# A hybrid decoder layer on one core: the 24 gate tiles shared out between sample attention, prompt attention and recurrent block

## The reference

```python
p = _split_proj(jnp.einsum('btd,de->bte', h, lw['w_in']) + lw['b_in'])
o_a = nsa(...)       # compressed, selected and window attention, 8 heads
o_b = _rglru(...)    # recurrent block: conv, gates, scan over time
o_c = _gla(...)      # gated linear attention

def _merge(o_a, o_b, o_c, gate_pre, w_branch, w_out):
    u = jnp.einsum('btzc,zcd->btzd', jnp.stack([o_a, o_b, o_c], axis=2), w_branch)
    g = jax.nn.sigmoid(gate_pre.reshape(B, T, N_BRANCH, D_MODEL))
    return jnp.einsum('btd,de->bte', jnp.sum(g * u, axis=2), w_out)

def _mlp(h, w1, w2):
    a = jax.nn.relu(jnp.einsum('btd,df->btf', h, w1))
    return jnp.einsum('btf,fd->btd', a * a, w2)
```

## Time and profile before

| | us |
|---|---|
| median of 3 runs (2349.26 to 2356.98) | 2355.3 |
| the profiled execution, its own time | 2354.62 |
| its span | 2353.0 |
| TensorE busy | 2128.4 (90%) |
| VectorE busy | 852.0 (36%) |
| ScalarE busy | 694.6 (30%) |
| GpSimd busy | 330.6 (14%) |

### The profile page before, as it was taken

The page is one execution under the profiler, slowest core; times in us unless marked ns, Lnnn a source line. Parts: engine busy times, 40 slices in busy tenths (PEclk is TensorE's granted clock), DMA queues, the critical chain, the costliest instruction groups (busy, mean ns, idle before and its releaser), DMA issues. The chain is left out here.

```text
span 2353.0 us, 36411 instructions
## 1 busy us (share of the span) xinstructions
PE 2128.4 (90%) x14280; PEld 1439.2 (61%) x14280; DVE 852.0 (36%) x1636; ACT 694.6 (30%) x1279; POOL 330.6 (14%) x245
## 2 busy tenths in 40 slices
PE   3888966799999999897699979895999999999998
PEld 2446634577777777664366756563666666666666
DVE  4211051455555555455432544334222222222223
ACT  5212231245454545326142233212211111211121
POOL 3200032400000000000102111102510410411400
PEclk7898978899999999898799989996999999999999
DMA  5421352111111111201110155302111111111101
GB/s 207 127 71 46 128 149 71 49 50 43 55 38 56 55 47 38 74 23 36 38 45 9 63 145 151 134 12 54 45 54 45 53 48 50 45 53 45 53 27 74
DMA packets 189719, 153.31 MB, mean 65 GB/s; under 512 B 9169, under 2 KB 176231, under 8 KB 189291
## 3 DMA queue, kind: packets, MB, share of 16 engines
q1 hardware_dynamic: 180170, 138.96, 19.6%
q0 software_dynamic: 4640, 10.60, 1.7%
q10 hardware_dynamic: 4800, 2.30, 0.3%
HBM read 124.66 MB, written 31.33 MB: 66 GB/s over the span
## 5 line engine op out<-in xcount | busy, mean ns | idle before, releaser
L416 PE MATMUL ps<-hH,wH 128*128 128x352 f16 x1536 | 318.3, 317 | 47.7 <-ACTq L389 27.8
L416 PE MATMUL ps<-hL,wH 128*128 128x352 f16 x1536 | 317.5, 316 | 0.0
L416 PE MATMUL ps<-hH,wL 128*128 128x352 f16 x1536 | 316.5, 315 | 0.0
L403 DVE SCALAR_TENSOR_TENSOR wL<-w,wH 128x1024 f16<-128x1024 f32 x98 | 120.1, 1225 | 323.8 <-ACT wH L396 308.3
L416 PEld LDWEIGHTS ps<-hH,wH 128*128 128x128 f16 x1536 | 151.4, 99 | 132.8 <-issue 48.5
L416 PE MATMUL ps<-mH,wH 128*128 128x352 f16 x960 | 195.9, 313 | 8.4 <-DVEq L389 6.9
L416 PEld LDWEIGHTS ps<-hL,wH 128*128 128x128 f16 x1536 | 152.1, 99 | 82.1
L416 PEld LDWEIGHTS ps<-hH,wL 128*128 128x128 f16 x1536 | 151.7, 99 | 81.3
L416 PE MATMUL ps<-mL,wH 128*128 128x352 f16 x960 | 195.9, 313 | 0.0
L416 PE MATMUL ps<-mH,wL 128*128 128x352 f16 x960 | 195.9, 313 | 0.0
L485 PE MATMUL ps<-hH,wH 128*128 128x352 f16 x576 | 181.0, 314 | 2.0 <-ACT cmpT L497 0.8
(11 more groups left out here) (409 smaller groups left out, 2929.3 us busy)
## 6 DMA issues: line engine op xcount, KB each, us to landing
w<-in_mlp_w SPq DMA_DIRECT2D x64, 512.0 KB, 3.9
w<-in_w_in SPq DMA_DIRECT2D x32, 512.0 KB, 3.9
gates<-cmpT SPq DMA_DIRECT2D x24, 528.0 KB, 3.0
hH<-gates SPq DMA_DIRECT2D x24, 528.0 KB, 3.5
paw<-in_w_in SPq DMA_DIRECT2D x24, 512.0 KB, 4.7
hL<-in_w_branch SPq DMA_DIRECT2D x24, 256.0 KB, 3.8
xTd<-xT SPq DMA_DIRECT2D x1, 4224.0 KB
xT<-xTd SPq DMA_DIRECT2D x1, 4224.0 KB, 13.0
```

Source lines behind the costliest of these rows:

```text
L403: self.k.nc.vector.scalar_tensor_tensor(self.k.wL[:, slot % 2, :, :], self.k.w32[:, slot, :, :], WS, self.k.wH[:, slot % 2, :, :], ALU.mul ...
L416: ins = nc.tensor.matmul(k.ps[:, 3 * parity + c, 0:CH], w[:, kt, :], x[:, kt, c * CH:(c + 1) * CH], start=(kt == 0 and x is inH and w is w ...
```

## The change

The 24 gate tiles are divided: tiles 0 to 3 are a `Fill` in `sample_attention`, tiles 4 to 19 the `Fill` of `prompt_attention`, and tiles 20 to 23 become four more tiles of the `Dense` of `lru`.

In `sample_attention` the fill's raw weights lie in the buffer of `k.toep` (the table of the relative bias), so the load of `toep` moves from `project_nsa` to the end of `sample_attention`. TensorE issues 4 fills after each group of key transposes, a chunk of 24 at each of the two waits for the softmax, one (first half) or two (second half) chunks ahead of the value products, and one after the first half's value products. ScalarE splits the first two tiles ahead of its first key copy; VectorE makes their low halves ahead of its other preparations. Bank 6 is now the fill's, so the small transposes go to the end of bank 7.

In `prompt_attention` the pieces follow the slots' sizes: `even_pieces` gives slot j a piece so that 3 x (tiles of jobs j, j + 2, j + 4) + 4 x piece is nearly level, and a piece never goes past a chunk's end. The pieces are 0 to 20 matmuls: the first 48 slots are 11, 10, 3, 18, 6, 13, 9, 2, 17, 7, 9, 9, 6, 9, 8, 7, 7, 6, 7, 4, 8, 5, 6, 5, 5, 5, 4, 4, 5, 1, 7, 4, 4, 3, 4, 2, 4, 3, 4, 2, 3, 3, 2, 3, 2, 8, 5, 8.

In `lru` the gate tiles are staged in the free part of `oH` and `oL` and stored by SyncE; the linear attention's ScalarE waits for these stores before it overwrites that part. SyncE loads the block-diagonal weights `gw` earlier, and `load_ahead` of the next stage and the four small outputs stand behind evictions of the gate tiles.

```diff
@@ sample_attention
+        raw = k.toep[:, :, :].rearrange("p h n -> p (h n)").rearrange("p (s kt n) -> p s kt n", s=2, kt=KD)
+        fill = Fill(k, "sf", 0, FILL_SAMPLE, raw, k.cmpT, 6)
+        PIECE, CHUNK = KD // 2, 3 * KD
...
+            fill.load(sp, 0)
+            fill.load(sp, 1)
             for b in range(NB):
+                if b == 4:
+                    fill.load(sp, 2)
+                    fill.load(sp, 3)
+                if b == NB - 1:
+                    fill.store(sp, 0)
...
+            fill.store(sp, 1)
+            sp.wait_ge(fill.lo, FILL_SAMPLE)
+            sp.dma_start(k.toep[:, :, :], ...).then_inc(s["toep"], 16)
+            for i in range(2, FILL_SAMPLE):
+                fill.store(sp, i)
+            fill.all_stored(sp)
+            sp.wait_ge(s["toep"], 16)
@@ TensorE
                         ins.then_inc(s["kturn"], 1)
+                        fill.multiply(pe, PIECE)
...
+                fill.multiply(pe, CHUNK)
                 pe.wait_ge(s["csoft"], hf + 1)
...
+                fill.multiply(pe, CHUNK)
                 pe.wait_ge(s["ccopy"], hf + 1)
...
+                fill.multiply(pe, CHUNK * (hf + 1))
                 pe.wait_ge(val_in[hf], 16 * (9 - VA) * HS)
...
                 ins.then_inc(s["o"], 1)
+                if not hf:
+                    fill.multiply(pe, CHUNK)
@@ ScalarE
+                    if b == 0:
+                        fill.split_hi(act, 0)
+                        fill.split_hi(act, 1)
+                    elif b == HS:
+                        fill.evacuate(act, 5)
...
+                    if b % 2:
+                        fill.evacuate(act, 6 * hf + b % HS // 2)
+                    if b == HS:
+                        fill.split_hi(act, 3)
                 act.wait_ge(s["cprep"], 2 * hf + 2)
...
+                fill.evacuate(act, 6 * hf + 2)
+                if not hf:
+                    fill.split_hi(act, 2)
@@ prompt_attention
-    PIECES = ((8, 0), (8, 0), (8, 1), (8, 0), (8, 0), (8, 1), (12, 0), (12, 1))
+def even_pieces(tiles, chunks, size):
+    total, level = chunks * size, 0
+    while sum(max(0, level - 3 * n) for n in tiles) < 4 * total:
+        level += 1
+    pieces, at, due = [], 0, 0.0
+    share = total / sum(max(0, level - 3 * n) for n in tiles)
+    for n in tiles:
+        due += share * max(0, level - 3 * n)
+        piece = max(0, min(round(due) - at, size - at % size))
+        pieces.append(piece)
+        at += piece
...
-                        fill.multiply(pe, PIECES[(j - LEAD) % 8][0])
+                        fill.multiply(pe, pieces[j - LEAD])
@@ lru
+                for m in range(MT - 1):
+                    sp.wait_ge(dn.evacuated, 2 * MT + m + 3)
+                    sp.dma_start(k.gates[gate0 + m], staged[m]).then_inc(k.gates_kept, 16)
                 sp.wait_ge(dn.lo, n)
                 nxt.load_ahead(sp)
+                sp.wait_ge(dn.evacuated, 2 * MT + MT + 2)
+                sp.dma_start(k.gates[gate0 + MT - 1], staged[MT - 1]).then_inc(k.gates_kept, 16)
                 sp.wait_ge(s["pout"], 1)
...
+                    if i >= 2 * MT:
+                        act.wait_ge(s["prod"], m + 1)
+                        nc.scalar.copy(k.oH[:, 4 + m, :], gg[:, m, :]).then_inc(s["hi"], 1)
                     dn.wait_tile(act, i)
...
                     one_less_square(m)
+                    if m == 1:
+                        dn.split_lo(dve, 2 * MT, 0)
                 settle(nc.vector.memset(a5[:, :, 0:1], 0.0))
                 for m in range(MT):
+                    if m:
+                        dn.split_lo(dve, 2 * MT + m, m)
...
+                    if i == n - 2:
+                        pe.wait_ge(s["pack"], MT)
+                        for u in range(MT):
+                            ins = nc.tensor.transpose(k.ps[0:36, 7, u * P:(u + 1) * P], pack[:, u, :], k.c('ident'))
```

105 lines of the change are left out of this document (64 added, 41 removed).

## The result

| | before | after |
|---|---|---|
| median, us (after: 4 runs, 2314.45 to 2323.09) | 2352.3 | 2315.4 |
| ratio, 95% interval | | 0.985 [0.9826, 0.9873] |
| span of the profiled execution | 2353.0 | 2312.8 |
| sample attention, first bias load to first score of the prompt attention | 125.9 | 143.1 |
| prompt attention, first score to last combine | 541.3 | 467.2 |

What follows compares the result with a forecast made beforehand. TensorE was taken as the bound, with no free time in the prompt attention and plenty in the two other stages. -73 (prompt) + 21 (sample) + 18 (recurrent) = -34 us from 2355.3 gave 2321 us, range 2300 to 2346.

Steps and rivals of the forecast that it cites:

- The bound, and the fill's price: Prompt attention: TensorE has no free time; 576 gate matmuls at 0.149 us taken away save 85.8 us.
- The 13 us that the prompt attention keeps: Prompt attention: 7 us of eviction waits plus 6 us of combine waits, leaving -73 of the -85.8 us.
- The wait for the bank: Prompt attention: next chunk waits for ScalarE's eviction of the fill's one PSUM bank, 0.15 us for each of 48 chunks, 7 us.
- The 6 us for the combine: Prompt attention: value products share one bank and wait for VectorE's combine of the slot before, 6 us in all (0 to 10).
- A sign that fits by its ends: Signs of being right: sample attention 143 us long; idle TensorE in the prompt attention up by some 13 us.
- Sample attention: Four tiles added there, 42.9 us of matmuls, partly hidden under waits: +21 us, ends +4 and +34.
- Start: Sample attention start: late weights and two splits ahead of ScalarE's first key copy, plus slow first fills: +10 us.
- the two -2: Sample attention: fills replace waits, so a warmer TensorE clock saves 2 us in each half.
- Recurrent block: Four tiles added at its end, `pack` just hidden, next stage near 1155.7 instead of 1138.0: +18 us, ends +14 and +24.
- GpSimd as the pace: Sample attention: GpSimd's page loads stay the pace, so the stage costs only +2; total 2302 us, chance 0.12.
- Hand-offs: Prompt attention: hand-offs replace TensorE as bound, 0.15 us more for each of 192 slots, 29 us; 2350 or 2342, chance 0.15.
- Round trip: Prompt attention: score-to-exponential round trip paces all slots, losing 0.35 us each (67 us); slower, 2375 us, chance 0.08.

Runs made afterwards that it cites:

- without the scraps: Changed kernel, but a piece takes the rest of its chunk where fewer than five matmuls would be left: 2314.6 us, ratio 0.9834.
- the combined kernel: Changed kernel with six fills in every prompt attention slot, later start of the sample attention's fill, shorter end of the recurrent block: 2299.1 us, ratio 0.9775.

## Why the prediction was right, step by step

- **The bound, and the fill's price.** 0.149 us for each of 576 matmuls, 85.8 us: borne out by the run with six fills a slot, which gave back 84.6. The 131 ns a pair of the Trainium skill (TensorE: Matmul & The Clock Gate, Back-to-back issue gap), quoted beside it, would have made 75 us at most, less than was measured; the row was the better guide.
- **The 13 us that the prompt attention keeps.** The sum was right (-73 forecast, -74.1 measured), its inside was not, and that the two agree to 1 us is luck. The wait for the bank was named, with its mechanism, and its row is near the 7 us booked (6.4 to 7.6), but in 15 waits rather than 0.15 us in each of 48; by the starts of the matmuls the chunks' first fills cost 9.1 us more than with six a slot. The 6 us for the combine were 1.2. In their place stand that larger wait and the copies, some 2 us behind 22 weight loads, a hand-off that the prediction named only in a rival ("ScalarE's transposed copies all wait on TensorE today, which hides their length"). What failed inside is the step that put all this down to the fill being thinner ("What is late once the fill is thinner?"): thinner in equal pieces costs 1 us, and dividing the thin fill by slot size 10.5 more. The prediction saw that small slots follow each other and that many chunks end in them, and took the 0.15 us from there, but booked nothing that another division would have saved.
- **A sign that fits by its ends.** "That stage is 143 us" was the 122 us from 310 to 432 plus 21. By those ends the stage took 139; the 143.1 of the table is counted to the first score of the prompt attention, where it was 125.9 before. "Idle TensorE up by some 13" was 7 in the view (6.7 to 13.7), for the reason given with the waits: a short wait does not show as idle time.
- **Sample attention.** +17.1 for +21. Start: +10.2 at the gate matmul (27.6 us after the stage's start before, at 337.75, and 37.8 after, at 348.24) for +10; of it 6.8 stand ahead of the first key copy (2.5 and 9.4), for 7.5. Value products of the first half +11.6 from the stage's start, for 11.2 forecast (10 + 1.9 + 1.3 - 2). The chunk ahead of the next key transposes +2.2 for 2.3, the wait for the split 2.37 for 2.4. From the first half's last transpose to the second half's value products +6.6, where 2.4, 6 and 1, less 1 for the clock, make 8.4: the fills among the key transposes cost less than 6. And the value products of the first half run 1.9 us shorter, the stretch behind the start of the second half's 1.4, on top of what the transposes gain: warm matmuls were worth a little more than the two -2. TensorE, not a transfer, ended the wait for both groups, as said.
- **Recurrent block.** +16.1 for +18. `pack` just hidden, as said (no wait, pitch of the products 8.8 us for 8.7 forecast). The end was 5.3 us after the last matmul where 6.3 was booked (1149.4 to 1155.7); the other microsecond is within what this stretch varies.
- **The load of `toep`, GpSimd, the linear attention's wait for the gates:** nothing, as said.
- **Rivals.** GpSimd as the pace: out, no value product waited for a page. Hand-offs: the waits are there, but within the 13 us already booked and not 29 more, and in equal pieces the bank's and the copies' are nearly gone with the same 16 tiles, while 5.7 us for the combine are left. Round trip: score matmuls waited for an exponential 4.2 us in 2 waits after, 3.3 before; out. With a division that leaves one fill in every fourth slot the prompt attention is 14.4 us above the best, which is half way to the hand-off rival's 29.

So the forecast came out 6 us high, all of it in the two added stages; the prompt attention's sum held because the 10.5 us of the division stood in it under another name.

## What to carry to other kernels

- Filler work hides the hand-offs of the slots it stands in. Try equal pieces, and chunks that end where pieces end, before levelling the slots' lengths: here pieces of 6 beat pieces by slot size by 11 us of 2315.
- Work added to a stage with idle engines was dearest at the start, where it stood ahead of the first link of the chain; starting it one step later made the stage 5 us shorter.
- A row of waits on a weight load is not time lost on TensorE, and a short wait may not show as idle time at all. Check it by the distance of the starts.
- When a sum comes out right, undo its parts once: here one run changed the cause, and showed where the next 11 us were.

## What the runs showed that was not expected

**The granted clock falls after one and the same short wait in some executions and not in others.** In the second half of the sample attention TensorE waits 2.4 us for VectorE's split of tile 2. Stretches around that wait (384 to 400) and two more of the same stage, the run with six fills a slot (us; busy of PE, PEld, DVE, ACT, POOL; granted clock; DMA):

```profile
339.20:342.50 3.30, 3.30 (x19) 2.04 (x18) 0.00 (x0) 1.12 (x2) 1.31 (x3) 0.50 1.14 347
...
384.00:390.00 6.00, 3.64 (x27) 2.42 (x26) 2.77 (x10) 1.13 (x2) 2.14 (x4) 1.00 0.12 33
390.70:394.20 3.50, 3.50 (x21) 2.20 (x20) 0.00 (x0) 1.17 (x2) 1.72 (x4) 0.57 0.18 42
394.20:400.00 5.80, 5.36 (x31) 2.60 (x28) 0.91 (x1) 2.00 (x3) 2.01 (x4) 1.00 0.71 204
...
427.90:431.20 3.30, 3.30 (x15) 1.82 (x13) 0.00 (x0) 0.84 (x2) 0.00 (x0) 0.50 0.00 0
```

The changed kernel, at the same place:

```profile
383.00:389.00 6.00, 3.63 (x29) 2.83 (x27) 2.60 (x9) 1.91 (x4) 2.03 (x5) 1.00 0.15 44
389.00:399.00 10.00, 9.35 (x51) 3.96 (x49) 1.22 (x1) 3.55 (x6) 3.96 (x7) 1.00 0.53 152
```

The busy times ahead are alike (3.64 and 3.63 of 6 us). In the one the clock goes to its lower level (1.2 GHz; fills 0.29 us apart instead of 0.15) within 1.3 us after TensorE has gone back to work (389.52), and stays there for some 3 us while it is busy without a gap; in the other it stays at 2.4 GHz. Two more such falls stand in the same stage of the first execution: at 339, behind a wait of 2.09 us for the fill's bank, and at 428, behind three waits of 0.2 to 0.7 us. The changed kernel had 1.00 all the way from 325 to 447 us. Over the whole sample attention the mean clock was 0.93 in the changed kernel and 0.91 with six fills a slot, and the stages 143.1 and 147.5 us; half speed in three stretches of 3.3 us (the second within the third row) gives an estimate of 5 us lost, about the difference. The rest of the way to the linear attention goes roughly with the clock too: 172.4 us at a mean of 0.97 (pieces of 8, 8, 7, 1), 176.7 at 0.96 (the changed kernel), 179.7 at 0.94 (six a slot), with the same code there. A stage with short idle stretches thus has no single length, and two profiled executions compared there can differ by 4 to 7 us with the same code. Why the clock falls in one execution and not in another is not shown. The Trainium skill (TensorE: Matmul & The Clock Gate, A second HAM failure mode) describes a clock that goes back and forth through short idle times between groups of matmuls, there through waits on PSUM banks; the fall at 339 agrees, the one at 390 stands behind a wait for weights.

What stays open: why ScalarE's eviction comes late for the first fill of a chunk also behind larger pieces (4.3 us without the scraps), which no run took away while keeping pieces by size, and whether the combined kernel's total is 4 us above the sum of its parts at all.
